# A hybrid SSD and attention block: the step size made ahead of the modulation, and one convolution tap moved to ScalarE

## The reference, cut to what matters

```python
proj = h @ w_in
z, xbc, dt_raw = proj[..., :i0], proj[..., i0:i1], proj[..., i1:i2]   # 512, 768 and 8 columns
xbc_c = silu(causal_conv(xbc, conv_prev, conv_w, conv_b))             # 4 taps, each shifted by one row
dt = softplus(dt_raw + dt_bias)
A = -exp(a_log)
y, h_fin = ssd_scan(xs * dt[..., None], dt * A, Bm, Cm, h0)           # xs, Bm, Cm are parts of xbc_c
y = (y + d_skip * xs) * silu(z)
logf = log_sigmoid(f_raw + f_bias)                                    # 8 columns, for the attention mixer

def causal_conv(xbc, prev, w, b):
    xpad = concatenate([prev, xbc], axis=1)
    out = b + xpad[:, 0:L] * w[0]
    for i in range(1, 4):
        out = out + xpad[:, i:i + L] * w[i]
```

## Time and profile before

| | |
|---|---|
| median of 3 runs | 2657.5 us (2654.47 to 2658.01) |
| the profiled execution | 2658.54 us, of which the span of the trace is 2656.9 us |
| busy over the span | TensorE 2294.4 us, VectorE 1413.5 us, ScalarE 945.0 us, GpSimd 711.0 us |
| mean granted TensorE clock | 0.926 |
| the SSD stage in the trace | about 60 to 554 us |

### The profile page before, as it was taken

How to read it: one execution, slowest core, us unless ns; L and a number is a source line. 1 busy time by engine, 2 the same in 40 slices (tenths; PEclk the granted TensorE clock), 3 DMA queues, 4 the chain that set the end, 5 groups by cost and what they waited for, 6 DMA issues and landing times. The chain is left out here.

```text
span 2656.9 us, 35209 instructions
## 1 busy us (share of the span) xinstructions
PE 2294.4 (86%) x11464; PEld 1778.9 (67%) x11465; DVE 1413.5 (53%) x2903; ACT 945.0 (36%) x1628; POOL 711.0 (27%) x753
## 2 busy tenths in 40 slices
PE   3898989759999879999996799839999999999860
PEld 1788878646778745556653677628888888888650
DVE  2688788761110056666663567752445562435656
ACT  2445444321111125555555334321233441223533
POOL 0000001000000047777775002122223332223220
PEclk8999999879999969999998899959999999999885
DMA  6411111147674294444533544253667884656657
GB/s 218 159 67 71 67 71 56 51 171 280 219 261 167 101 206 87 87 86 89 111 61 106 177 148 143 100 199 83 182 186 239 276 263 130 181 152 212 228 190 269
DMA packets 190369, 408.39 MB, mean 154 GB/s; under 512 B 65306, under 2 KB 72776, under 8 KB 186848
## 3 DMA queue, kind: packets, MB, share of 16 engines
q1 hardware_dynamic: 160976, 304.44, 35.6%
q0 software_dynamic: 26672, 93.99, 12.8%
q10 hardware_dynamic: 2624, 8.72, 0.8%
HBM read 296.57 MB, written 110.53 MB: 153 GB/s over the span
## 5 line engine op out<-in xcount | busy, mean ns | idle before, releaser
L1381 POOL TENSOR_TENSOR c_acc<-c_acc,c_pr 128x512 f32<-128x512 f32 (+3 forms) x320 | 340.1, 1063 | 76.0 <-ACT c_pr L1503 35.3
L1503 ACT ACTIVATE c_pr<-c_ps,neg_f 128x512 f32<-128x512 f32 (+2 forms) x360 | 208.0, 595 | 162.5 <-PE c_ps L1447 156.2
L1533 DVE TENSOR_REDUCE c_mx<-c_pm 128x1 f32<-128x512 f32 (+3 forms) x304 | 178.9, 613 | 58.0 <-PE c_pm L1403 40.2
L1403 PE MATMUL c_pm<-c_km,c_q 66*128 66x512 f32 (+1 forms) x336 | 144.9, 448 | 22.3 <-DMA c_km<-f_k 16.1
L258 PE MATMUL p_zx<-wa_hi,ah_hi 128*128 128x432 f32 x408 | 155.5, 381 | 3.6 <-DVE ah_lo L640 3.6
L258 PE MATMUL x_pg<-x_g_hi,x_x_hi 128*128 128x512 f32 x336 | 136.2, 405 | 24.8 <-DVE x_x_lo L2467 24.8
L1456 PE MATMUL c_po<-c_pr,c_vv 128*64 128x512 f32 (+3 forms) x720 | 151.4, 522 | 0.0
L607 POOL TENSOR_TENSOR yskip<-xs,params 128x512 f32<-128x512 f32 x17 | 21.5, 1266 | 482.8 <-ACT xs L545 482.8
L259 PE MATMUL p_zx<-wa_lo,ah_hi 128*128 128x432 f32 x408 | 150.2, 368 | 0.0
L260 PE MATMUL p_zx<-wa_hi,ah_lo 128*128 128x432 f32 x408 | 149.1, 365 | 0.0
L258 PE MATMUL x_pd<-x_d_hi,x_m_hi 128*128 128x512 f32 x344 | 140.8, 409 | 6.8 <-DVE x_m_lo L2477 6.8
(11 more groups left out here) (393 smaller groups left out, 5519.2 us busy)
## 6 DMA issues: line engine op xcount, KB each, us to landing
x_raw_g<-in_w_gate_dram SPq DMA_DIRECT2D x32, 1024.0 KB, 8.0
x_raw_u<-in_w_up_dram SPq DMA_DIRECT2D x32, 1024.0 KB, 10.2
x_raw_d<-in_w_down_dram SPq DMA_DIRECT2D x32, 1024.0 KB, 7.9
b_wa<-in_w_ada_dram POOLq DMA_DIRECT2D x16, 1024.0 KB, 7.0
c_k<-k_hi SPq DMA_DIRECT2D x14, 672.0 KB, 13.7
h_hi<-ah_hi SPq DMA_DIRECT2D x17, 512.0 KB, 2.6
h_lo<-ah_lo SPq DMA_DIRECT2D x17, 512.0 KB, 3.5
d_mix<-mix SPq DMA_DIRECT2D x17, 512.0 KB
```

Of the source, the lines that this page charges most:

```text
L1381: pool.tensor_tensor(acc[:, ci % 2, cols], acc[:, ci % 2, cols], pr[:, i % RING, cols], ALU.add).then_inc(acc_done, 1)
L1403: last = pe.matmul(p_m[x % 2][:, 0:w * P], q2[0:KR, s, u["tile"] * P:(u["tile"] + 1) * P], km[:, s, kc], start=True, stop=not masked)
L1503: act.activation(pr[:, n % RING, cols], p_s[n % NPS][:, cols], ACT.Exp, bias=c.neg_f[:, it["h"], it["key"]:it["key"] + 1]).then_inc(exp_do ...
L1533: dve.tensor_reduce(mx[:, u % 2, pc["slot"]:pc["slot"] + 1], src, AX.X, ALU.max).then_inc(mx_done, 1)
```

## The change

The order of the weights' columns becomes dt, gates, z, xbc, so that the 16 small columns lie in the first third of `zx` (`DTF` is 16). They are loaded by two small DMAs ahead of the large one, where there was one small one behind it.

VectorE makes dt, dA and `lf` as soon as `mm` is done, ahead of its half of the modulation, and no longer after the state. ScalarE runs the two small functions after the first and after the second third of `zx`.

ScalarE also takes the unshifted tap of the convolution with the bias straight out of `p_h`, in six instructions behind `xraw`, and signals `conv_first`. VectorE adds the other three taps in 18 instructions and waits for `conv_first` where it waited for `xraw_ready`; so does TensorE ahead of L429, which overwrites `p_h`.

```diff
-    chunks = [[(0, CA + H, a["w_in"][0][k * P:(k + 1) * P, 0:CA + H]),
-               (CA + H, WA, a["w_in"][0][k * P:(k + 1) * P, C_F:C_F + H])] for k in range(KD)]
+    rows = lambda k, lo, hi: a["w_in"][0][k * P:(k + 1) * P, lo:hi]
+    chunks = [[(0, H, rows(k, CA, CA + H)), (H, DTF, rows(k, C_F, C_F + H)), (DTF, WA, rows(k, 0, CA))] for k in range(KD)]
...
@@ TensorE, step @@
-                    pe.wait_ge(xraw_ready, i)
+                    pe.wait_ge(conv_first, i)
...
@@ ScalarE, step @@
                         act.activation(zx[:, g * GW:(g + 1) * GW], p_zx[:, g * 512:g * 512 + GW], ACT.Copy).then_inc(zx_ready, 1)
+                        if g == 0:
+                            act.wait_ge(dt_step, i * 9 + 3)
+                            act.activation(t16[:, 3, :], t16[:, 2, :], ACT.Exp, scale=-1.0).then_inc(dt_exp, 1)
+                        elif g == 1:
+                            act.wait_ge(dt_step, i * 9 + 4)
+                            act.activation(t16[:, 5, :], t16[:, 4, :], ACT.Ln).then_inc(dt_ln, 1)
                 if nxt:
                     modulate(i, group)
                 if front:
                     act.wait_ge(zx_ready, i * 3 + 3)
-
-                    act.wait_ge(dt_step, i * 9 + 3)
-                    act.activation(t16[:, 3, :], t16[:, 2, :], ACT.Exp, scale=-1.0).then_inc(dt_exp, 1)
-                    act.wait_ge(dt_step, i * 9 + 4)
-                    act.activation(t16[:, 5, :], t16[:, 4, :], ACT.Ln).then_inc(dt_ln, 1)
                     act.wait_ge(xbc_T, i + 1)
                     if back:
                         act.wait_ge(carried, i)
                     act.activation(xraw[:, :, CW - 1:], p_hv[:, 0:NC, :], ACT.Copy).then_inc(xraw_ready, 1)
+                    for q in range(NC):
+                        last = act.activation(conv[:, q, :], p_hv[:, q, :], ACT.Identity, bias=c.vcol[:, V_CB + q:V_CB + q + 1],
+                                              scale=c.vcol[:, V_CW + NC * (CW - 1) + q:V_CW + NC * (CW - 1) + q + 1])
+                    last.then_inc(conv_first, 1)
...
@@ VectorE, step @@
-                    dve.wait_ge(xraw_ready, i)
+                    dve.wait_ge(conv_first, i)
...
-                    for t in range(CW):
+                    for t in range(CW - 1):
                         for q in range(NC):
...
-                            if t == 0:
-                                ins = dve.tensor_scalar(conv[:, q, :], src, w, c.vcol[:, V_CB + q:V_CB + q + 1], ALU.mult, ALU.add)
-                            else:
-                                ins = dve.scalar_tensor_tensor(out=conv[:, q, :], in0=src, scalar=w, in1=conv[:, q, :], op0=ALU.mult, op1=ALU.add)
+                            ins = dve.scalar_tensor_tensor(out=conv[:, q, :], in0=src, scalar=w, in1=conv[:, q, :], op0=ALU.mult, op1=ALU.add)
...
+                if front:
+                    dve.wait_ge(zx_ready, i * 3 + 1)
...
                 if nxt:
                     modulate(i, group)
...
-                if front:
-
-
-                    dve.wait_ge(zx_ready, i * 3 + 3)
```

More of the change, by code:

```diff
@@ L260, in product3 @@
     return pe.matmul(out, a_lo, b_hi, start=False, stop=stop)
+DTF = 2 * H
 def ssd_weights(nc, ctx, a):
-    chunks = [[(0, CA + H, a["w_in"][0][k * P:(k + 1) * P, 0:CA + H]),
-               (CA + H, WA, a["w_in"][0][k * P:(k + 1) * P, C_F:C_F + H])] for k in range(KD)]
+    rows = lambda k, lo, hi: a["w_in"][0][k * P:(k + 1) * P, lo:hi]
+    chunks = [[(0, H, rows(k, CA, CA + H)), (H, DTF, rows(k, C_F, C_F + H)), (DTF, WA, rows(k, 0, CA))] for k in range(KD)]
     return chunks, [ctx.enter_context(nc.sbuf_tensor(n, [P, KD, WA], F32R)) for n in ("wa_hi", "wa_lo")]
@@ L317, in ssd_branch @@
             "ssm0_copied"))
-        skip_ready, wb_loaded = sem("skip_ready"), sem("wb_loaded")
+        skip_ready, wb_loaded, conv_first = sem("skip_ready"), sem("wb_loaded"), sem("conv_first")
         block = ctx.enter_context(nc.Block())
@@ L375, in _ @@
             sp.wait_ge(zx_ready, 3 * LAST)
-            sp.dma_start(a["conv_prompt"][0, 0], zx[P - CW + 1:P, DS:CA]).then_inc(conv_out, 16)
+            sp.dma_start(a["conv_prompt"][0, 0], zx[P - CW + 1:P, DTF + DS:]).then_inc(conv_out, 16)
             sp.wait_ge(carried, LAST)
@@ L381, in _ @@
             step(LAST, nxt=False)
-            sp.dma_start(a["conv_sample"][0, 0], zx[DEC - CW + 1:DEC, DS:CA]).then_inc(conv_out, 16)
+            sp.wait_ge(zx_ready, 3 * LAST + 3)
+            sp.dma_start(a["conv_sample"][0, 0], zx[DEC - CW + 1:DEC, DTF + DS:]).then_inc(conv_out, 16)
             ssm_store(1, a["ssm_prompt"])
@@ L471, in step @@
                     for q in range(NC):
-                        last = pe.transpose(p_h[:, q * P:(q + 1) * P], zx[:, DS + q * P:DS + (q + 1) * P], c.ident[:])
+                        last = pe.transpose(p_h[:, q * P:(q + 1) * P], zx[:, DTF + DS + q * P:DTF + DS + (q + 1) * P], c.ident[:])
                     last.then_inc(xbc_T, 1)
@@ L534, in step @@
                     act.wait_ge(y_ready, i)
-                    act.activation(zs[:], zx[:, 0:DS], ACT.Silu).then_inc(zs_ready, 1)
+                    act.activation(zs[:], zx[:, DTF:DTF + DS], ACT.Silu).then_inc(zs_ready, 1)
                     act.wait_ge(conv_ready, i)
@@ L645, in step @@
                 if back:
-                    dve.wait_ge(xraw_ready, i)
+                    dve.wait_ge(conv_first, i)
                     if isinstance(i, int) and i == NT:
                         dve.wait_ge(conv_in, 16 * NC)
-                    if not (isinstance(i, int) and i == 1):
-                        dve.wait_ge(xbc_ready, i - 1)
-                    for t in range(CW):
+                    for t in range(CW - 1):
                         for q in range(NC):
@@ L654, in step @@
                             src = xraw[:, q, t:t + P]
-                            if t == 0:
-                                ins = dve.tensor_scalar(conv[:, q, :], src, w, c.vcol[:, V_CB + q:V_CB + q + 1], ALU.mult, ALU.add)
-                            else:
-                                ins = dve.scalar_tensor_tensor(out=conv[:, q, :], in0=src, scalar=w, in1=conv[:, q, :], op0=ALU.mult, op1=ALU.add)
-                        ins.then_inc(conv_step if t < CW - 1 else conv_ready, 1)
+                            ins = dve.scalar_tensor_tensor(out=conv[:, q, :], in0=src, scalar=w, in1=conv[:, q, :], op0=ALU.mult, op1=ALU.add)
+                        ins.then_inc(conv_step if t < CW - 2 else conv_ready, 1)
                         if nxt and t == 0:
                             mean_square(i)
-                        if t < CW - 1:
-                            dve.wait_ge(conv_step, i * 3 + t - 1)
+                        if t < CW - 2:
+                            dve.wait_ge(conv_step, i * 2 + t)
                     dve.wait_ge(conv_ready, i)
@@ L689, in step, with small @@
                     last.then_inc(m_ready, 1)
+                if front:
+                    dve.wait_ge(zx_ready, i * 3 + 1)
+                    n = 0
+                    def small(build):
+                        nonlocal n
+                        n += 1
+                        build().then_inc(dt_step, 1)
+                        dve.wait_ge(dt_step, i * 9 + n)
+                    t = lambda s: t16[:, s, :]
+                    small(lambda: dve.tensor_tensor(t(0), zx[:, 0:DTF], c.params[:, 0:2 * H], ALU.add))
+                    small(lambda: dve.tensor_tensor(t(1), t(0), c.sign[:], ALU.mult))
+                    small(lambda: dve.scalar_tensor_tensor(out=t(2), in0=t(1), scalar=-1.0, in1=t(1), op0=ALU.mult, op1=ALU.max))
+                    dve.wait_ge(dt_exp, i + 1)
+                    small(lambda: dve.tensor_scalar(t(4), t(3), 1.0, None, ALU.add))
+                    small(lambda: dve.scalar_tensor_tensor(out=t(6), in0=t(4), scalar=-1.0, in1=t(3), op0=ALU.add, op1=ALU.subtract))
+                    small(lambda: dve.reciprocal(t(7), t(4)))
+                    small(lambda: dve.tensor_tensor(t(8), t(6), t(7), ALU.mult))
+                    dve.wait_ge(dt_ln, i + 1)
+                    small(lambda: dve.tensor_tensor(t(9), t(5), t(8), ALU.subtract))
+                    small(lambda: dve.scalar_tensor_tensor(out=t(0), in0=t(1), scalar=0.0, in1=t(9), op0=ALU.max, op1=ALU.add))
+                    if back:
+                        dve.wait_ge(lf_stored, i * 16)
+                    dve.tensor_scalar(lf[:], t(0)[:, H:2 * H], -1.0, None, ALU.mult)
+                    rows = slice(0, P)
+                    if isinstance(i, int) and i == LAST:
+                        dve.memset(dt[DEC:P, :], 0.0)
+                        dve.memset(dA[DEC:P, :], 0.0)
+                        rows = slice(0, DEC)
+                    dve.tensor_copy(dt[rows, :], t(0)[rows, 0:H])
+                    dve.tensor_tensor(dA[rows, :], t(0)[rows, 0:H], c.neg_a[rows, :], ALU.mult).then_inc(dt_ready, 1)
                 if nxt:
```

## The result

The changed kernel takes 2597.0 us (median of 4 runs, 2593.87 to 2600.66) against 2656.3 us for the kernel before in the same comparison: a ratio of 0.9777, 95% interval 0.976 to 0.9794. The forecast was 2599 us. The profiled execution took 2597.99 us for a span of 2595.8.

A forecast was written before the change was run, and what follows sets the result against it. No engine was full: a chain around VectorE and TensorE, each waiting once for the other, set the tile. 49.4 plus 10.8 less 1.5 gave 58.7 us off 2658.5, so 2600, median 2599; range 2588 to 2620.

The forecast's parts named there:

- The loop: 13 tiles of the first stage fall from 26.6 to 22.8 us each, a gain of 49.4 us.
- the ends: Steps 15, 16 and 17 of the stage gain 4.2, 5 (3 and 2) and 1.6 us: together 10.8 us.
- the loads: A second small load per weight slice, issued ahead of the large one, costs 1.5 us, bounds 0 and 4.8.
- The wait also costs clock: TensorE's wait for dA lowers its granted clock: 0.95 over the 13 tiles, 1.00 where it came without a pause.
- VectorE's circle: One tile of VectorE's work without its waits, from modulation round to the next: 22.4 us.
- the small ones end about when the turn does: VectorE's small instructions, 2.59 us behind mm, finish about when TensorE has turned the next input.
- TensorE's circle: One tile of TensorE's own work at the upper clock without its wait: 22.6 to 22.8 us.
- The forecast's own lower end: 2590 us: no wait at all, 22.4 us a tile and nothing lost at the loads.
- The tap: Six ScalarE instructions, 2.3 us, hidden with 1.4 us of margin; VectorE's convolution falls from 6.76 to 5.2 us.
- the second and third rivals: Second: ScalarE's tap comes onto the path, 2611 us, chance 0.06. Third: taps far longer, slower than before, 2669, chance 0.04.
- The first rival: Small instructions end behind the turn and push modulation, state and TensorE: 24.2 us a tile, 2618 us, chance 0.12.
- The fourth: Rival of no change: the wait for dA becomes an equal wait for xbc, 2655 us, chance 0.04.

The follow-up runs named there:

- e5: The changed kernel with projection 2's third product left out, eight matmuls less for TensorE in a tile: 2572.5 us, ratio 0.9681.
- e1: The changed kernel with the whole convolution back on VectorE, the small instructions staying moved: 2606.5 us, ratio 0.9808.
- e2: The changed kernel with the small instructions back behind the state and their two ScalarE functions ahead of xraw and the tap: 2674.4 us, ratio 1.0059.
- e8: Against e2, the two small functions put behind the tap in ScalarE's queue: 2648.4 us, ratio 0.9967.
- e4: The changed kernel with each weight slice's large load put ahead of its two small ones: 2596.3 us, ratio 0.9766.
- e7: The changed kernel with the large weight loads first and the sample's load no longer waiting for the clearing of other rows: 2590.6 us, ratio 0.9739.
- e3: The changed kernel with six more ScalarE activations of the tap's form, into a tile nothing reads, ahead of the tap: 2596.9 us, ratio 0.9769.

## Why the prediction was right, and where its working was not

**The mechanism held.** The small instructions left the link from the state to TensorE, the 32.7 us of waits for dA went, TensorE runs without a gap at the upper clock, and its own work is the tile: 22.65 us where 22.8 was forecast. The loop gave 51.2 us for a term of 49.4. That the time is within 2 us of the forecast is in part luck: the loop, the ends and the loads came out 1.8, 1.3 and 1.3 us better than their terms, 4.3 together by the stage's end (63.0 for 58.7), and 1.9 of that is lost again in the untouched stages.

"The wait also costs clock" holds for nine tiles of thirteen only, and is the smaller part: 0.65 us of the 3.93. The 2.97 us that the prediction set beside its 2.17 come from such a tile.

**The step that was mis-sized is VectorE's circle.** "Together 22.4 us" is 21.39 (e5). Nearly all of it is the 8.25 us from modulation to state and the 0.19 behind it, 7.58 in e5, where VectorE is not early: 0.79 us of the stretch that I read in the earlier trace rows is a wait of the low part for ScalarE's rounding, a wait counted as work:

```profile
325.50 1.29 DVE L640 TENSOR_TENSOR ah_lo<-h,ah_hi 128x512 fp32r<-128x512 f32 x2 [0.79 <-ACT ah_hi L524]
```

So "the small ones end about when the turn does" is off too: they end 0.55 us ahead of VectorE's next start, the idle time ahead of the modulation averages 8.6/15 = 0.57 us, just over the 0.5 announced, and the reserve is 1.26 us, not 0.3. It did not move the forecast because TensorE's circle, which I took, was the longer by either size; it did spoil my expectations of e1 and e5. (The forecast's own lower end, with 22.4 us a tile and no loss at the loads, comes to 2592 by its terms, not 2590.)

**The tap** is hidden with 1.3 us to spare (1.4 forecast), and six took 2.20 us (2.3 forecast). The Trainium skill, "ScalarE: Activation LUTs", section "Rules for kernel authors", would have left it on VectorE, and the trace agrees that it is dearer on ScalarE, 2.20 against 1.66 us. But e1 is the change without it, and it is slower (2606.5 against 2597.0 us): with the small instructions moved, VectorE is the engine without room (23.20 us against 22.65), and ScalarE the one with it. In e2, where ScalarE's taps come late, they do cost: the place of the second and third rivals, though by the order of the queue (e8) and not by the taps' length. What kept it away is that the change also moves the two small functions, so that they no longer stand ahead of the tap in ScalarE's queue (e8). The halves are worth 52.1 us (e1) and -15.8 us (e2) alone, and 59.3 together (2656.3 - 2597.0). With e8's 7.3 in place of e2's loss they would add up, to 59.4; but e8 gains its part elsewhere, in TensorE's wait for xbc and in step 15, so that may be chance.

**The ends** gave 12.1 us for a term of 10.8. Step 15 gave 5.7 where 4.2 was reckoned (its parts, 1.7 and 2.6, make 4.3); the rest, 6.4, stands against 6.6.

**The loads.** The weights' split, first start to last end, went from 17.5 us to 19.6 in the changed kernel, and to between 19.2 and 20.8 in the experiments that keep its order of loads, so the term of 1.5 was 0.2 to 1.8 us too small (single executions each). In the total it is not seen: the first projection began at 71.24 us instead of 71.64, where 1 to 2 us later was announced, and step 1 came only 0.2 us later, since the split began at 39.65 instead of 41.92 us in that execution, and the start varies by more (37.0 to 42.6 in these runs) than the term. The order of the loads accounts for a part of it: with the large load first the split took 18.46 (e4) and 18.63 us (e7), less than in any run with it last. What the rest is stays open.

**The first rival**, circles that do not mesh, did not happen, and e1 shows how near it was without the tap. The fourth, a wait for xbc in place of the one for dA, is seen in the loop of e1, with 0.28 us. The kernel before had one of 0.62 to 0.66 in the four tiles whose clock stayed up, behind the wait for dA; the change has neither.

## What to carry to other kernels

When two engines form a circle, take each engine's own length without the waits that shrink when it is late; the surest way to read it is a run in which the other engine does less. The price of work moved to an idle engine was set here by what stood ahead of it in that engine's queue, and hardly by its duration (e3): the same six instructions were worth -16 us (e2), +7 (e8) and, in the change against e1, 7 to 10 (59.3 - 52.1, or 2606.5 - 2597.0). Two moves can need one another, so the parts' times alone need not add up to the whole: 52.1 and -15.8 do not make 59.3.

## What was not expected of the hardware

An elementwise instruction of VectorE (two inputs, both in SBUF) took 0.69 or 1.53 us with the same operands, by whether GpSimd had started its product first. The timelines of the kernel before, GpSimd and then VectorE:

```profile
317.72 1.21 POOL L607 TENSOR_TENSOR yskip<-xs,params 128x512 f32<-128x512 f32 x1 [23.83 <-ACT xs L545]
...
317.95 1.53 DVE L683 TENSOR_TENSOR xdt<-xs,dt 128x512 f32<-128x512 f32 x1
```

and of the changed kernel:

```profile
264.18 0.69 DVE L687 TENSOR_TENSOR xdt<-xs,dt 128x512 f32<-128x512 f32 x1
...
264.22 1.55 POOL L616 TENSOR_TENSOR yskip<-xs,params 128x512 f32<-128x512 f32 x1 [20.10 <-ACT xs L549]
```

Whoever starts second is the longer one. It is not the version that decides: before, one tile of the loop had the other order and an xdt of 0.69 us (at 371.65, GpSimd 0.04 behind), and in e5, a version of the change, GpSimd is 0.08 us ahead and xdt takes 1.53. The Trainium skill, "SBUF — State Buffer", section "Who interferes with whom", says that a VectorE instruction with two SBUF inputs contends with a GpSimd one that reads SBUF, that the port pair they share is an exclusive lock, and that issue order decides who blocks. VectorE's row agrees: GpSimd ends at 318.93, xdt 0.55 us later, somewhat less than its 0.69 alone. GpSimd's row agrees in part: it ends 0.90 us behind xdt, less than its 1.21. In the changed kernel the shorter xdt brings little, as mm then waits 0.66 us for ScalarE's seg.
